# A fused float32 transformer program on one core: GpSimd's sums moved apart, an earlier split, a row of norm weights, and a last feed-forward finished in quarters

## The reference

```python
def modulate(h, shift, scale):
    return h * (1.0 + scale[:, None, :]) + shift[:, None, :]

def swiglu(h, w_gate, w_up, w_down):
    return (jax.nn.silu(h @ w_gate) * (h @ w_up)) @ w_down

def even_layer(x, c, ada_w, ada_b, ...):        # odd_layer: the same around stick-breaking attention
    sh_m, sc_m, g_m, sh_f, sc_f, g_f = ada_modulation(c, ada_w, ada_b)
    h = modulate(rms_norm_2(x, mix_norm), sh_m, sc_m)
    ...
    x = x + g_m[:, None, :] * y
    hf = modulate(rms_norm_2(x, ffn_norm), sh_f, sc_f)
    return x + g_f[:, None, :] * swiglu(hf, ffn_w_gate, ffn_w_up, ffn_w_down)
```

## Time and profile before

| | |
|---|---|
| median of three runs | 887.36 us |
| the profiled execution's own time | 887.93 us |
| its span from first to last instruction | 886.1 us |
| what lies around the span | 1.8 us |
| PE busy | 875.6 us |
| VectorE (DVE) busy | 711.1 us |
| ScalarE (ACT) busy | 492.2 us |
| GpSimd (POOL) busy | 94.1 us |

### The profile page before, as it was taken

One profiled execution on the slowest core, in us unless ns is written; L12 is line 12 of the kernel. 1 busy time (PEld: TensorE's weight loads), 2 busy tenths in 40 slices (PEclk: granted clock), 3 DMA queues, 4 the chain that ended last, 5 costly groups with the idle time before them and its releaser, 6 DMA issues.

```text
span 886.1 us, 13231 instructions
## 1 busy us (share of the span) xinstructions
PE 875.6 (99%) x4809; PEld 741.3 (84%) x4809; DVE 711.1 (80%) x730; ACT 492.2 (56%) x667; POOL 94.1 (11%) x74
## 2 busy tenths in 40 slices
PE   9999999999999999999999999999999999999998
PEld 5998878888888799879888888877777888888886
DVE  5698977988888987998998998689797865655655
ACT  6545665565556657755454455554676365545542
POOL 4000110000000104126101500034000100000000
PEclk9999999999999999999999999999999999999999
DMA  7989585899999484547999698545434376666661
GB/s 233 336 261 340 183 301 180 324 357 372 332 327 334 146 285 152 169 157 227 331 365 322 241 363 300 174 140 194 141 119 125 97 249 196 189 190 189 190 193 69
DMA packets 117096, 208.07 MB, mean 235 GB/s; under 512 B 7237, under 2 KB 81069, under 8 KB 111930
## 3 DMA queue, kind: packets, MB, share of 16 engines
q1 hardware_dynamic: 116566, 205.31, 68.3%
q10 hardware_dynamic: 292, 2.10, 0.7%
q0 software_dynamic: 192, 0.05, 0.0%
HBM read 206.39 MB, written 1.05 MB: 234 GB/s over the span
## 4 chain that ended last, share of the span: by engine, by line
PE 86%; DVE 8%; issue 2%; ACT 2%; DMA 1%; POOL 0%; DVEq 0%; SPq 0%; ACTq 0%; POOLq 0%
PE ub L1910 10%; PE tp L1910 10%; PE acc L1788 7%; PE acc L1789 7%; PE acc L1791 7%; PE ub L1912 5%; PE tp L1912 5%; PE acc L1751 5%; PE acc L1753 4%; PE acc L1752 4%; DVE w_lo L1158 3%; PE acc L1896 2%; PE acc L1898 2%; PE acc L1897 2%; PE tp L1973 2%
## 5 line engine op out<-in xcount | busy, mean ns | idle before, releaser
L1158 DVE TENSOR_TENSOR w_lo<-w_raw,w_hi 128x1024 fp32r<-128x1024 f32 x274 | 346.7, 1282 | 84.5 <-ACT w_hi L735 83.8
L735 ACT ACTIVATE w_hi<-w_raw 128x1024 fp32r<-128x1024 f32 x274 | 286.5, 1056 | 206.6 <-PE acc L1791 41.3
L1910 PE MATMUL tp<-aT,w_hi 128*128 128x512 f32 x432 | 135.9, 396 | 0.0
L1910 PE MATMUL ub<-aT,w_hi 128*128 128x512 f32 x432 | 135.4, 395 | 0.0
L1788 PE MATMUL acc<-w_hi,hT_hi 128*128 128x512 f32 x272 | 106.3, 391 | 1.1 <-DVE w_lo L1158 1.1
L1789 PE MATMUL acc<-w_lo,hT_hi 128*128 128x512 f32 x272 | 105.9, 389 | 0.0
L1791 PE MATMUL acc<-w_hi,hT_lo 128*128 128x512 f32 x264 | 102.7, 389 | 0.0
L1912 PEld LDWEIGHTS tp<-aT,w_lo 128*128 128x128 f32 x432 | 81.1, 188 | 19.2
L1912 PEld LDWEIGHTS ub<-aT,w_lo 128*128 128x128 f32 x432 | 81.1, 188 | 18.9
L1912 PE MATMUL tp<-aT,w_lo 128*128 128x256 f32 x432 | 84.9, 278 | 0.0
L1912 PE MATMUL ub<-aT,w_lo 128*128 128x256 f32 x432 | 84.9, 278 | 0.0
(11 more groups left out here) (321 smaller groups left out, 1399.4 us busy)
## 6 DMA issues: line engine op xcount, KB each, us to landing
ada_raw<-in_l_ada_w SPq DMA_DIRECT2D x24, 1024.0 KB, 7.2
w_raw<-in_l_ffn_w_gate SPq DMA_DIRECT2D x44, 512.0 KB, 4.6
w_raw<-in_l_ffn_w_up SPq DMA_DIRECT2D x44, 512.0 KB, 4.5
w_raw<-in_l_ffn_w_down SPq DMA_DIRECT2D x44, 512.0 KB, 4.1
w_raw<-in_w_up SPq DMA_DIRECT2D x32, 512.0 KB, 5.0
w_raw<-in_w_down SPq DMA_DIRECT2D x32, 512.0 KB, 5.6
scratch<-in_l_ada_w SPq DMA_DIRECT2D x14, 1024.0 KB, 7.8
w_raw<-in_attn_w_qkv SPq DMA_DIRECT2D x24, 512.0 KB, 6.9
```

Source lines behind the costliest of these rows:

```text
L735: act.activation(rounded_part(v), w_raw[:, v % SLOTS, :], ACT.Copy).then_inc(hi_done, 1)
L1158: dve.tensor_tensor(rest_part(v), w_raw[:, v % SLOTS, :], rounded_part(v).bitcast(F32), ALU.subtract).then_inc(lo_done, 1)
L1910: pe.matmul(banks[f], rounded_part(v)[:, c[f]], aT[:, :, b, :], start=b == 0, stop=False)
```

## The change

Five things. (1) GpSimd's sums: those of GATE_F of layer 0 move from the mixer to the start of the first gated feed-forward; the four of `mod_next` are cut into two at that place and two later, one every two slices; the four of the second third are spaced by one slice each; of the four in the last mixer the two of G_F move six parts later with two parts between them, and the two of GATE_F go into the last feed-forward. The memset and bias DMA of the last third stand behind four of the sums and get a semaphore of their own; step K moves behind P15. (2) In the last slice of the first gated feed-forward the last held part is split, on ACT and DVE, ahead of the copy and sum of the up product. (3) The first norm's weights come as one row by one DMA; DVE clears a tile, copies the two halves of the row into it, and PE spreads them with full 128-row products; one warming product ahead and the one behind are gone; ACT splits the second weight part ahead of the first copy of transposes. (4) In the last feed-forward the k=1 block of tile 1 is left to the end (`last_left` is `(1,)` for layer 1). (5) The last tile's second half is closed early: DVE adds what is summed by then, and the last three blocks go to `ub` as two quarters of 256 columns, each multiplied, added and written out by itself.

```diff
@@ -89,7 +89,7 @@
-    P9 T1 B1 H13 L13 P10 K0 H14 L14 P11 Q2 R2 N2 H15 L15 P12 H16 L16 P13 T2 B2 H17 L17 P14 H18 L18 P15 Q3 R3 N3 H19
+    P9 T1 B1 H13 L13 P10 H14 L14 P11 Q2 R2 N2 H15 L15 P12 H16 L16 P13 T2 B2 H17 L17 P14 H18 L18 P15 K0 Q3 R3 N3 H19
@@ -602,7 +606,8 @@
-            parts = [(t, slice(c * CH, (c + 1) * CH)) for t in range(NT) for c in range(2)]
+            parts = [(t, slice(c * CH, (c + 1) * CH)) for t in range(NT) for c in range(2)][:3]
+            parts += [(1, slice(c * TOK, (c + 1) * TOK)) for c in (2, 3)]
@@ -619,12 +624,12 @@
-            def start_sums(layer, third, dst=None):
+            def start_sums(layer, third, dst=None, done=ada_bias):
...
-                pool.dma_start(dst[0:1, :], ada_b[layer][:, c]).then_inc(ada_bias, 16)
+                pool.dma_start(dst[0:1, :], ada_b[layer][:, c]).then_inc(done, 16)
@@ -692,21 +697,25 @@
             partition_sums(G_F, G_F, w_used, parts_to(U_WIN + 5), 2)
-            partition_sums(GATE_F, gate_ffn, w_used, parts_to(U_WIN + 7), 2)
...
-            start_sums(1, 2)
-            partition_sums(mod_next, mod[:, 0:UNIT], ada_used, 24, 0)
-            partition_sums(mod[:, UNIT:2 * UNIT], mod[:, UNIT:2 * UNIT], ada_used, 32, 0)
+            partition_sums(GATE_F, gate_ffn, ada_used, 24, 0)
+            partition_sums(mod_next[:, 0:D], mod[:, 0:D], ada_used, 24, 0)
+            pool.wait_ge(pool_sum, 4)
+            start_sums(1, 2, done=ada_bias_last)
+            partition_sums(mod_next[:, D:UNIT], mod[:, D:UNIT], w_used, parts_to(U_SG0 + 12), 12)
+            partition_sums(mod[:, UNIT:2 * UNIT], mod[:, UNIT:2 * UNIT], ada_used, 32, 2)
...
-            partition_sums(mod[:, 2 * UNIT:3 * UNIT], mod[:, 2 * UNIT:3 * UNIT], w_used, parts_to(U_QKV2 + 2), 0)
+            partition_sums(G_F, G_F, w_used, parts_to(U_QKV2 + 5), 2)
...
+            pool.wait_ge(xn_done, 24)
+            partition_sums(GATE_F, GATE_F, w_used, parts_to(U_SG1 + 8), 6)
@@ -822,7 +831,7 @@
-            act.dma_start(gain[0:P:P // 2, 0, 0:CH], gains[0].rearrange("(a n) -> a n", a=2)).then_inc(gain_loaded[0], 16)
+            act.dma_start(gain[0:1, 0, :], gains[0].rearrange("(a n) -> a n", a=1)).then_inc(gain_loaded[0], 16)
@@ -837,8 +846,8 @@
                         split_part(2 * u)
+                        split_part(2 * u + 1)
...
-                        split_part(2 * u + 1)
@@ -1076,9 +1085,13 @@
                     split_part(2 * v + 6, i, 6)
+                    held_last = not layer and i is None and j == NJ_SG - 1
+                    if held_last:
+                        split_part(2 * v + 7)
...
-                    split_part(2 * v + 7, i, 6)
+                    if not held_last:
+                        split_part(2 * v + 7, i, 6)
@@ -1286,14 +1299,20 @@
+                dve.wait_ge(w_used, 2 * u_end - 3)
+                gated(1, g_mod, 1).then_inc(last_half, 1)
...
-                dve.wait_ge(w_used, parts_to(u_end))
-                gated(1, g_mod, 1).then_inc(x_ready, 1)
+                dve.wait_ge(last_half, 1)
+                for c, done, count in ((2, quarter_done, 1), (3, w_used, parts_to(u_end))):
+                    part = slice(c * TOK, (c + 1) * TOK)
+                    dve.wait_ge(done, count)
+                    chained(dve.tensor_tensor(xn[:, 1, part], ub[:, c - 2, 0:TOK], g_mod[:, part], ALU.mult))
+                    dve.tensor_tensor(x[:, 1, part], x[:, 1, part], xn[:, 1, part], ALU.add).then_inc(x_ready, 1)
@@ -1373,6 +1392,10 @@
+            chained(dve.memset(gain[:, 1, :], 0.0))
+            dve.wait_ge(gain_loaded[0], 16)
+            for n in range(2):
+                dve.tensor_copy(gain[0:1, 1, n * CH:(n + 1) * CH], gain[0:1, 0, n * CH:(n + 1) * CH]).then_inc(gain_row, 1)
@@ -1657,9 +1684,11 @@
                 one(u + 2, 1)
-                if layer == 0:
-                    dve.wait_ge(ada_bias, 96)
...
+                    if layer == 0 and third == 0:
+                        dve.wait_ge(ada_bias, 80)
+                    elif layer == 0:
+                        dve.wait_ge(ada_bias_last, 16)
@@ -1727,7 +1756,7 @@
                 elif step == "K":
-                    ada_gain(1, 4, pool_sum, 16)
+                    ada_gain(1, 4, pool_sum, 14)
@@ -1791,8 +1821,24 @@
+            def last_tile(parts):
...
+                for out, c, width, begin, done in ((acc[:, 2, :], 0, CH, False, half_done),
+                                                   (ub[:, 0, 0:TOK], 2, TOK, True, quarter_done),
+                                                   (ub[:, 1, 0:TOK], 3, TOK, True, None)):
+                    cols = slice(c * width, (c + 1) * width)
+                    for v, k in parts:
+                        op_hi, op_lo = hT_hi[:, k, P:TOK], hT_lo[:, k, P:TOK]
+                        pe.matmul(out, op_hi, rounded_part(v)[:, cols], start=begin and v == parts[0][0], stop=False)
+                        pe.matmul(out, op_hi, rest_part(v)[:, cols], start=False, stop=False)
+                        last = pe.matmul(out, op_lo, rounded_part(v)[:, cols], start=False, stop=v == parts[-1][0])
+                        if done is None:
+                            last.then_inc(w_used, 1)
+                    if done is not None:
+                        last.then_inc(done, 1)
...
-                     left=()):
+                     left=(), tail=False):
@@ -1816,6 +1862,9 @@
                     lo(0, 1, 1).then_inc(tile0_done, 1)
+                    if tail:
+                        last_tile([(2 * u - 1, 2 * (1 - h) + 1)] + [(2 * u + k, 2 * h + k) for k in range(2)])
+                        return
@@ -2136,12 +2186,11 @@
-            warm_up(3)
-            pe.wait_ge(gain_loaded[0], 16)
+            warm_up(2)
...
-                q = slice(n * P // 2, n * P // 2 + 1)
-                pe.matmul(acc[:, 2 + n, :], ones[q, :], gain[q, 0, 0:CH], start=True, stop=True).then_inc(gain_spread, 1)
-            warm_up(1)
+                pe.wait_ge(gain_row, n + 1)
+                pe.matmul(acc[:, 2 + n, :], ones[:, :], gain[:, 1, n * CH:(n + 1) * CH], start=True,
+                          stop=True).then_inc(gain_spread, 1)
@@ -2314,7 +2363,8 @@
                     pe.wait_ge(hT_lo_done, plus(j0 + j, i, 2))
-                    down(v + 2, (j - 1) % 2, i, 6, first=j == 1, left=last_left if i is None and j == NJ_SG - 1 else ())
+                    down(v + 2, (j - 1) % 2, i, 6, first=j == 1, left=last_left if i is None and j == NJ_SG - 1 else (),
+                         tail=layer == 1 and i is None and j == NJ_SG - 1)
```

More of the change, by code:

```diff
@@ L2325, in swiglu @@
                 if layer:
[L2326 removed]
+                    down(u + 3 * NJ_SG - 1, (NJ_SG - 1) % 2, lo_count=j0 + NJ_SG, final=True, tail=True)
                 else:
```

14 lines of the change are left out of this document (10 added, 4 removed).

## The result

The changed kernel takes 890.02 us (median; before in the same comparison 887.45), a ratio of 1.0028 (95% interval 1.0019 to 1.0037): slower by 0.3%, clear of the noise, where 882.8 was forecast. One of the nine runs of each kernel took far longer (2237 us, and 957 before) and is left out of the ratio. The profiled execution has a span of 887.6 us (886.1 before).

The account below looks back on a forecast made before the run. PE, busy 875.6 of 886.1 us, was taken as the bound, losing time at waits for DVE, first product and end. Terms 1.0 - 1.3 + 0.47 + 0.7 + 1.9 + 1.2 + 0.6 = 4.6 give 887.36 - 4.6 = 882.8 (880.6 to 885.2).

Parts of the forecast that it names:

- Head: Program start: weight row, fewer warming products and ACT's new order bring the first real products sooner, gain 1.2 (0 to 1.9).
- Last mixer: Last mixer: PE's waits of 0.85 and 1.08 go as sums move, gain 1.9 (0.9 to 1.93).
- slower: First gated feed-forward: each sum holds DVE its whole 3.4 us, loss 6.6, total 888.1 or 889.7; chance 0.05.
- Sums out of the recurrent mixer: Layer 0's mixer: without GATE_F's sums PE's wait of 1.03 at 368.76 goes, gain 1.0 (0.5 to 1.03).
- Entry of the first gated feed-forward: Start of that feed-forward: four sums each hold a DVE split 2.04, so PE waits near 420, loss 1.3 (0 to 2.3).
- the sums at 408.4: First gated feed-forward: library loading starts at 400.23 and takes 8.18, so sums start at 408.4 instead of 411.03.
- the entry costs nothing: First gated feed-forward: loading hides or DVE splits run between holds, the loss of 1.3 is absent, 881.5; chance 0.12.
- Later sums in the loop and the held split: Feed-forward: spaced sums recover 0.47 (0 to 0.47) at 500.87; splitting the held part sooner gains 0.7 (0.3 to 0.73) at 570.86.
- the second weight part's split ends at 8.9 ahead of the copy of the transposes: Program start, ACT: this 1.05 split, before at 10.03, moves ahead, bringing `xn` of tile 1 from 12.72 to about 11.5.
- the clock as a sign: Program start: TensorE's granted clock, with one warming product less, was named as a way the forecast could be wrong.
- The rival on GpSimd's memset beside the copies: Program start: DVE's row copies wait for GpSimd's memset (4.94 to 6.75), no gain, 884.0, or loss 0.4, 884.4; chance 0.12 to 0.13.
- End of the program: Last tile: quarters of 256 columns shorten the final DVE instructions and DMA, gain 0.6 (0.3 to 0.9).

Follow-up runs that it names:

- first three experiments: Changed kernel plus a small GpSimd iota at the end, 882.61 us; changed kernel, GATE_F's sums ahead of the last norm, 885.36; kernel before with only GATE_F's sums moved, 892.43.
- eighth experiment: Changed kernel plus a GpSimd iota at its end, with G_F's two last-mixer sums and step K back at their old places: 881.89 us.
- second experiment: Changed kernel with the last layer's two GATE_F sums ahead of the last norm's roots, so one library loading less: 885.36 us, ratio 0.9981.
- kernel with the iota: Changed kernel plus one small GpSimd iota behind the last two sums, so one more library loading at the end: 882.61 us, ratio 0.9946.

## Why the prediction was wrong

**The step that failed is one that was not there.** Under "Head" the forecast begins with GpSimd's `ident` as given, since AFFINE_SELECT stood at 1.77 in the trace of before. Under "Last mixer" it says of GATE_F's sums in the last feed-forward "nothing". Both are right by themselves, and the move connects them over the end of the program: it changes the library with which GpSimd begins. The term "Head" was a gain of 1.2; in its place stands a loss of 6.34 at the first product. The rows for it were at hand, since the order of GpSimd's instructions has a loading ahead of AFFINE_SELECT, the trace of before shows that it took no time there (the earlier trace rows show one that took 8.18), and the order of the changed kernel ends with sums. The first three experiments show it in both directions. The forecast did give "slower" a chance of 0.05, but for another mechanism, sums that hold DVE for their whole length, which did not come. (Its summary has 887.7 for that rival, where its own paragraph works out 888.1 to 889.7; nothing else hangs on it.) With a loading hidden at the end the changed kernel takes 882.61, against 882.8 forecast. That the agreement is so near is luck: two terms of about the same size, the entry's loss of 1.3 and the head's gain of 1.2, both came out near nothing.

**Sums out of the recurrent mixer**: 1.0 forecast, 1.02 gained at that wait and 1.02 lost again when undone. Right.

**Entry of the first gated feed-forward**: a loss of 1.3 forecast, 0.08 measured by the places in the changed kernel. The holds of 2.04, each meeting a split, were right ("Now every hold meets a split"). The step that failed is "the sums at 408.4", which takes the loading at 8.18 as fixed. In the changed kernel it took 6.79:

```profile
412.18 6.55 POOL L661 PARTITION_ALL_REDUCE gate_ffn<-mod  x2 [6.79 <-issue]
...
422.62 0.40 PE L1818 MATMUL acc<-w_hi,hT_hi 128*128 128x512 f32 x1
```

The sums start 10.4 ahead of the down product, not 417.47 - 408.4 = 9.1. My rival "the entry costs nothing" came true, by a shorter loading and not by what I had named. A start at 9.1 was not met by any run: at 10.4 the loss is 0.08, at 10.1 it is 0.37 and, in the eighth experiment, 0.31, at 7.1 it is 0.70. So the loss grows as the sums start later, as forecast, but no run shows the 1.3. The Trainium skill (page "SBUF — State Buffer", section "Who interferes with whom") says that the lock lasts a whole instruction. With holds as long as a sum, the prediction's own sequence takes 18.4 us from the first sum to D's end (408.4 to 426.8) and would put that end at 412.18 + 18.4 = 430.6 here, an estimate, 5.2 behind the need at 422.62 + 2.73 = 425.4. No wait of that kind is in any trace of this study.

**Later sums in the loop and the held split**: forecast 0.47 and 0.7, measured 0.47 and 0.56 (a loss of 0.17 from start to start stays at 574.55, where 0.73 was). Right, the second a little too high.

**Last mixer**: forecast 1.9, measured 2.1, of which both waits are 1.92. Right, but it was not the place that took the old waits away: with two sums instead of four at the old place they were gone in both experiments that had it.

**Head**, where the library is there: forecast a gain of 1.2, measured 0.0 by the medians, and in the traces 0.5 to 0.7 at full clock or a loss of 1.3 where the clock fell. The weight row comes even sooner than forecast (`xn` at 5.9 instead of 6.6). The step that failed is the one on ACT, "the second weight part's split ends at 8.9 ahead of the copy of the transposes": I priced the instruction and not its DMA. The split began at 8.34, the copy behind it at 9.31 and the product at 9.94, and in that execution TensorE's clock fell behind the wait. The prediction had named the clock as a sign, for a warming product less, and not for a wait. The rival on GpSimd's memset beside the copies was wrong in its place: they run from 2.21 to 3.75 in the kernel with the iota, before that memset. They took 1.54 for the two there and 0.75 in the changed kernel, where GpSimd stood still; GpSimd's two IOTAs beside them took 0.47 each, against 0.25 and 0.34 before. That fits what the Trainium skill (page "SBUF — State Buffer", section "Who interferes with whom") says of a DVE copy and a GpSimd instruction, that the later one waits, but no run takes them apart.

**End of the program**: forecast 0.6. The last product ends at 884.34 and the span 3.26 later, before 3.90 (from 882.22), so 0.64, less 0.11 for the products (2.12 late at their end, 2.01 ahead of the feed-forward): 0.5. Right. The last rows of DVE:

```profile
884.38 0.42 DVE L1314 TENSOR_TENSOR xn<-ub,mod 128x256 f32<-128x256 f32 x1
884.83 0.42 DVE L1315 TENSOR_TENSOR x<-x,xn 128x256 f32<-128x256 f32 x1
```

In all: gains of 4.85 where these terms (without the head) promised 3.4, the difference being mostly the entry's 1.3, and 6.34 lost at a place that I had priced at a gain.

## What to carry to other kernels

Look at the last instruction of each engine as you look at the first: what it leaves behind (here a library) is what the next execution starts with, and a loading that costs nothing in a trace may do so only for that reason. If a program must end with another library, load the first one again under cover of the last work. When an instruction is moved ahead on an engine, price the arrival of its data, and what waits behind it, before its own duration. The changed kernel with those two put right has the lowest median here, 881.68 us, and runs within 0.5 us of each other. And compare an execution's time with that of its kernel's other runs before you read a cause from its trace: the one trace here with a fallen clock behind the wait was the slowest of five.

## What the runs showed of the hardware

- A loading of GpSimd's library took 6.67 to 7.10 us ahead of the sums at the entry of the first gated feed-forward in the seven kernels where one memset and one bias DMA stand ahead of it, and 8.18, 9.11 and 9.58 in the three where two memsets do. The other library took 7.84 to 8.09 at the end of the six programs with the iota. At the start it took 11.67 and 12.11 us, and about nothing where the library was there. The DMA share was 0.87 to 0.94 in the nine of these stretches that were looked at, so it doesn't explain the difference; what does stays open. (The 9.12 us ahead of the sums in the last mixer, are no loading time: these sums start 0.2 us behind the end of the TensorE products that they wait for, in all three kernels with sums at that place.)
- That the library stays from one execution to the next is read from ten kernels: the two that end with sums start AFFINE_SELECT at 12.94 and 13.38, the eight that end with the other library at 1.75 to 1.77, whatever the number of loadings. No run looked at an execution behind another program, and none tells whether the library just stays or is put back at the start.
- A sum of GpSimd holds a scan of DVE for 2.04 us too (3.79 instead of 1.75), as it does splits.
- After 1.9 us without a product TensorE's granted clock was 0.61 of full speed over the next 4.4 us in one execution, and that cost 1.6 us against the second experiment's, with the same head. After 1.3 to 1.7 us without a product it stayed at 1.00, in four executions of kernels with the same head. In the changed kernel, where TensorE stood for 8.3 us, it was 0.68 from 14.7 to 20 us, yet by the places nothing more was lost behind the first product.
